# Last expert's output of a decoder layer sent off in two column halves, with first halves of four combine tiles loaded in between

## The reference, cut to what matters

```python
def run_block(args):                       # one block of 128 tokens of one expert
    tok, e = args
    xb = x_pad[tok]
    hb = jax.nn.silu(xb @ w_gate[e]) * (xb @ w_up[e])
    return hb @ w_down[e]
...
y = zeros.at[slot_tok].add(yb * slot_gate[:, None])
...
x = x + y                                  # then the final norm
return (rms_norm(yp, norm_final), rms_norm(ys, norm_final), ...)
```

## Time and profile before

| what | us |
|---|---|
| median of three runs | 1828.81 |
| lowest and highest run | 1828.12, 1834.88 |
| the profiled execution's own time | 1829.44 |
| span of its profile | 1827.8 |
| TensorE busy | 1767.3 (97%) |
| VectorE busy | 1152.3 (63%) |
| ScalarE busy | 860.0 (47%) |
| mean granted clock of TensorE | 0.983 of full speed |

### The profile page before, as it was taken

One profiled execution on the slowest core, in us unless ns is written; L12 is line 12 of the kernel. 1 busy time (PEld: TensorE's weight loads), 2 busy tenths in 40 slices (PEclk: granted clock), 3 DMA queues, 4 the chain that ended last, 5 costly groups with the idle time before them and its releaser, 6 DMA issues. The chain is left out here.

```text
span 1827.8 us, 28479 instructions
## 1 busy us (share of the span) xinstructions
PE 1767.3 (97%) x9926; PEld 1524.9 (83%) x9926; DVE 1152.3 (63%) x1954; ACT 860.0 (47%) x1554; POOL 486.5 (27%) x495
## 2 busy tenths in 40 slices
PE   7999999999999999999989999979999999999997
PEld 6878888999999788888879978768888888888882
DVE  5267666311111454545455556689999999999985
ACT  5255545311111233233232223358778777877873
POOL 3022332000000322323231112224955333332320
PEclk9999999999999999999999999979999999999998
DMA  7111212232222203030304643279999999999987
GB/s 233 48 48 47 55 47 55 86 94 70 81 70 82 66 16 92 26 92 23 95 2 143 199 146 111 85 306 386 391 389 385 392 384 384 386 381 390 384 335 291
DMA packets 149531, 333.30 MB, mean 182 GB/s; under 512 B 33712, under 2 KB 103008, under 8 KB 123792
## 3 DMA queue, kind: packets, MB, share of 16 engines
q1 hardware_dynamic: 127408, 278.19, 42.1%
q0 software_dynamic: 21376, 53.27, 8.4%
q10 hardware_dynamic: 672, 0.85, 0.3%
HBM read 304.24 MB, written 46.35 MB: 192 GB/s over the span
## 5 line engine op out<-in xcount | busy, mean ns | idle before, releaser
L2850 POOL DMA_INDIRECT y_d<-e_y,e_idxs x32 | 138.4, 4325 | 201.4 <-DVE e_y L2956 179.8
L2927 DVE TENSOR_TENSOR e_Lg<-e_rawg,e_Hg 128x1024 fp32r<-128x1024 f32 x128 | 148.2, 1219 | 8.3 <-ACT e_Hg L2876 8.3
L2927 DVE TENSOR_TENSOR e_Lu<-e_rawu,e_Hu 128x1024 fp32r<-128x1024 f32 x128 | 147.8, 1214 | 0.0
L2927 DVE TENSOR_TENSOR e_Ld<-e_rawd,e_Hd 128x1024 fp32r<-128x1024 f32 x124 | 143.1, 1214 | 0.0
L2876 ACT ACTIVATE e_Hg<-e_rawg 128x1024 fp32r<-128x1024 f32 x128 | 124.8, 1051 | 9.2 <-DMA e_rawg<-in_w_gate 9.2
L2876 ACT ACTIVATE e_Hu<-e_rawu 128x1024 fp32r<-128x1024 f32 x124 | 120.9, 1059 | 0.0
L2876 ACT ACTIVATE e_Hd<-e_rawd 128x1024 fp32r<-128x1024 f32 x124 | 120.8, 1051 | 0.0
L164 PE MATMUL bank<-r_wH,xH 128*128 128x512 f32 x256 | 105.3, 411 | 3.2 <-DVE r_gs L1530 3.2
L164 PE MATMUL bank<-e_Hg,e_xH 128*128 128x512 f32 x256 | 100.8, 394 | 3.6 <-DVE e_xL L2933 3.6
L164 PE MATMUL bank<-e_Hu,e_xH 128*128 128x512 f32 x256 | 102.8, 402 | 0.0
L166 PE MATMUL bank<-r_wH,xL 128*128 128x512 f32 x256 | 100.9, 394 | 0.0
(11 more groups left out here) (472 smaller groups left out, 4768.4 us busy)
## 6 DMA issues: line engine op xcount, KB each, us to landing
e_rawg<-in_w_gate SPq DMA_DIRECT2D x64, 1024.0 KB, 8.9
e_rawu<-in_w_up SPq DMA_DIRECT2D x64, 1024.0 KB, 7.7
e_rawd<-in_w_down SPq DMA_DIRECT2D x62, 1024.0 KB, 8.4
raw<-in_w_in SPq DMA_DIRECT2D x51, 512.0 KB, 4.0
c_Y<-y_d SPq DMA_DIRECT2D x8, 1024.0 KB, 12.6
m_t<-b_m_s POOLq DMA_DIRECT2D x8, 528.0 KB, 3.4
m_gate<-gate_t POOLq DMA_DIRECT2D x8, 528.0 KB, 3.9
m_m<-m_t POOLq DMA_DIRECT2D x8, 528.0 KB, 3.9
```

The lines of the kernel that those rows point to most:

```text
L2850: pool.indirect_dma_start(out=ch.y_d, out_offset=bass.IndirectOffsetOnAxis(ap=idx[:, e % IDX, 1:2], axis=0), in_=y[:], in_offset=None, bou ...
L2927: dve.tensor_tensor(L[kind][:, q], raw[kind][:, q], H[kind][:, q].bitcast(F32), ALU.subtract).then_inc(w_lo[kind], 1)
```

## The change

1. In the first stage, VectorE does `back(1)` before the bias sum of L423, and ScalarE waits for that sum and stores it one tile later.
2. `turn_hidden(31)` moves from behind `down(30)` to behind its first quarter; `hidden_hi(31)` and `hidden_lo(31)` move up with it, between the splits of the last down weights on VectorE. The split hidden rows of expert 31 lie in `xH`, `xL`.
3. The down product of expert 31 goes half by half into banks G and U: the 12 matmuls of the first 512 columns, then the 12 of the last.
4. VectorE computes two lists of row numbers (2r and 2r+1), and GpSimd scatters each half of `e_y` with an indirect DMA of its own (rows of 2 KB).
5. SyncE loads the first column halves of tiles 8, 0, 1 and 2 once the first half (and the scatter of expert 30) has landed, and after the second half their second halves and the five other tiles. Readers of those four tiles wait for both halves.

```diff
@@ stage_front, scalar
-                    if t == 1:
+                    if t == 2:
                         act.wait_ge(bias_sum, 1)
                         act.dma_start(ch.skew...)
@@ stage_front, vector
+                    back(t)
                     if t == 1:
                         dve.wait_ge(bias_mm, 1)
                         dve.tensor_tensor(ch.skew_rows[:], ...).then_inc(bias_sum, 1)
-                    back(t)
@@ class Combine
+    EARLY = (8, 0, 1, 2)
+    def landed(self, eng, t):
+        eng.wait_ge(self.y_in[t], 32 if t in self.EARLY else 16)
...
+        def load(t, cols):
+            m = rows_of(t)
+            sp.dma_start(self.Y[0:m, t, :, cols], ch.y_d[2 * t * P:2 * (t * P + m), cols].rearrange("(p k) d -> p k d", k=2)).then_inc(self.y_in[t], 16)
+        self.half_served(sp)
+        for t in self.EARLY:
+            load(t, slice(0, 512))
         self.served(sp)
         for t in self.ORDER:
-            sp.dma_start(self.Y[0:m, t], ch.y_d[...])
+            load(t, slice(512, D) if t in self.EARLY else slice(0, D))
@@ stage_experts
+        def hidden_at(e):
+            return (xH[:, 0:FT], xL[:, 0:FT]) if isinstance(e, int) and e == NE - 1 else (hH[:], hL[:])
...
         def served(eng):
             eng.wait_ge(y_st, 16 * NE)
+            eng.wait_ge(half_st, 16)
+        def half_served(eng):
+            eng.wait_ge(y_st, 16 * (NE - 1))
+            eng.wait_ge(half_st, 16)
...
+        sums_at = lambda e: (G, U) if isinstance(e, int) and e == NE - 1 else Y
@@ gpsimd
-                scatter(LAST)
+                pool.wait_ge(rows_done, 2)
+                for f, done, sent in ((0, y_a, half_st), (1, y_b, y_st)):
+                    pool.wait_ge(done, NE)
+                    pool.indirect_dma_start(out=ch.y_d.rearrange("r (f d) -> (r f) d", f=2), out_offset=...(ap=row2[:, f:f + 1], axis=0),
+                                            in_=y[:, f * 512:(f + 1) * 512], ...).then_inc(sent, 16)
@@ scalar
                 def out_evac(e):
-                    act.wait_ge(used["d"], e * NQ + 2 * NQ)
+                    if isinstance(e, int) and e == LAST:
+                        act.wait_ge(half_mm, 1)
+                    else:
+                        act.wait_ge(used["d"], e * NQ + 2 * NQ)
                     act.wait_ge(y_st, e * 16)
...
                         split_hi("g", NE)
+                        hidden_hi(NE - 1)
...
-                hidden_hi(NE - 1)
                 combine.diagonals(act)
@@ vector
+                def half_rows():
+                    dve.wait_ge(ch.e_idx_in[LAST % IDX], 16 * (LAST // IDX + 1))
+                    dve.tensor_copy(rowf[:], idx[:, LAST % IDX, 1:2]).then_inc(rows_done, 1)
+                    dve.wait_ge(rows_done, 1)
+                    dve.tensor_scalar(row2[:, 0:1], rowf[:], 2.0, None, ALU.mult)
+                    dve.tensor_scalar(row2[:, 1:2], rowf[:], 2.0, 1.0, ALU.mult, ALU.add).then_inc(rows_done, 1)
...
-                        split_lo("g", NE)
+                        split_lo("g", NE, range(NQ // 2))
+                        hidden_lo(NE - 1)
+                        half_rows()
+                        split_lo("g", NE, range(NQ // 2, NQ))
                     if not first:
                         out_evac(e - 1)
...
-                hidden_lo(NE - 1)
                 out_evac(NE - 1)
@@ tensor
-                def down(e, kind="d"):
+                def down(e, between=None):
...
+                        if q == 0 and between:
+                            between()
+                def down_halves(e):
+                    high, low = hidden_at(e)
+                    pe.wait_ge(h_lo, e + 1)
+                    for f in range(2):
+                        cols = slice(f * 512, (f + 1) * 512)
+                        for q in range(NQ):
+                            if f == 0:
+                                pe.wait_ge(w_lo["g"], NE * NQ + q + 1)
+                            mm = split_matmuls(pe, sums_at(e)[f][:], ...)
+                            if f == 1:
+                                mm.then_inc(used["d"], 1)
+                        if f == 0:
+                            mm.then_inc(half_mm, 1)
...
-                        down(e - 1)
+                        down(e - 1, between=None if left else lambda: turn_hidden(NE - 1))
...
-                turn_hidden(NE - 1)
-                down(NE - 1, "g")
+                down_halves(NE - 1)
```

More of the change, by code:

```diff
@@ L2617, with __init__ @@
     AHEAD = {0: 2, 2: 4, 6: 7}
-    def __init__(self, ch, sb, gain, served):
-        self.ch, self.gain, self.served = ch, gain, served
+    EARLY = (8, 0, 1, 2)
+    def __init__(self, ch, sb, gain, served, half_served):
+        self.ch, self.gain, self.served, self.half_served = ch, gain, served, half_served
         self.g_in, self.y_in, self.half, self.a_done, self.sq_done, self.ms_part, self.ms_done, self.root_done, self.rstd_done, self.o_done, self.o_st = (
@@ L2693, in weigh @@
             i = self.ON_DVE.index(t)
-            dve.wait_ge(self.y_in[t], 16)
+            self.landed(dve, t)
             dve.scalar_tensor_tensor(out=Y[:, t, 0], in0=Y[:, t, 0], scalar=gates[:, t, 0:1], in1=x2[:, t], op0=ALU.mult, op1=ALU.add).then_inc(self.half, 1)
@@ L2743, in experts @@
             m = rows_of(t)
-            pe.wait_ge(self.y_in[t], 16)
+            self.landed(pe, t)
             for f, bank in enumerate(self.halves(t)):
@@ L2786, in served @@
             eng.wait_ge(y_st, 16 * NE)
+            eng.wait_ge(half_st, 16)
+        def half_served(eng):
+            eng.wait_ge(y_st, 16 * (NE - 1))
+            eng.wait_ge(half_st, 16)
         end = ch.experts_at + 4 * 9 * NQ * 1024
         room = Room(nc, ch.experts_at, end)
-        combine = Combine(ch, room, rows, served)
+        combine = Combine(ch, room, rows, served, half_served)
         beyond = Beyond(ch, Room(nc, ch.experts_at, end), room, served)
@@ L2865, in _ @@
                         fill_beyond(e - 2)
-                scatter(LAST)
+                pool.wait_ge(rows_done, 2)
+                for f, done, sent in ((0, y_a, half_st), (1, y_b, y_st)):
+                    pool.wait_ge(done, NE)
+                    pool.indirect_dma_start(out=ch.y_d.rearrange("r (f d) -> (r f) d", f=2), out_offset=bass.IndirectOffsetOnAxis(ap=row2[:, f:f + 1], axis=0),
+                                            in_=y[:, f * 512:(f + 1) * 512], in_offset=None, bounds_check=4 * T - 1, oob_is_err=False).then_inc(sent, 16)
                 pool.wait_ge(scat2, 16 * 2 * NT)
@@ L2884, in hidden_hi @@
                     act.wait_ge(h_turned, e + 1)
-                    act.activation(hH[:].rearrange("p k i -> p (k i)"), HT[:], ACT.Copy).then_inc(h_hi, 1)
+                    act.activation(hidden_at(e)[0].rearrange("p k i -> p (k i)"), HT[:], ACT.Copy).then_inc(h_hi, 1)
                 def gate_sigmoid(e):
@@ L2892, in out_evac @@
                 def out_evac(e):
[L2893 removed]
+                    if isinstance(e, int) and e == LAST:
+                        act.wait_ge(half_mm, 1)
+                    else:
+                        act.wait_ge(used["d"], e * NQ + 2 * NQ)
                     act.wait_ge(y_st, e * 16)
[L2895 removed]
+                    act.activation(y[:, 0:512], sums_at(e)[0][:], ACT.Copy).then_inc(y_a, 1)
                 def body(e, first, left):
@@ L2923, in _, with split_lo @@
             def _(dve):
-                def split_lo(kind, e):
-                    for q in range(NQ):
+                def split_lo(kind, e, qs=range(NQ)):
+                    for q in qs:
                         dve.wait_ge(w_hi[kind], e * NQ + q + 1)
@@ L2937, in hidden_lo @@
                     dve.wait_ge(h_hi, e + 1)
-                    dve.tensor_tensor(hL[:].rearrange("p k i -> p (k i)"), HT[:], hH[:].rearrange("p k i -> p (k i)").bitcast(F32),
-                                      ALU.subtract).then_inc(h_lo, 1)
+                    high, low = (x.rearrange("p k i -> p (k i)") for x in hidden_at(e))
+                    dve.tensor_tensor(low, HT[:], high.bitcast(F32), ALU.subtract).then_inc(h_lo, 1)
+                def half_rows():
[4 more added lines that the diff above has]
+                    dve.tensor_scalar(row2[:, 1:2], rowf[:], 2.0, 1.0, ALU.mult, ALU.add).then_inc(rows_done, 1)
                 def gate_product(e):
```

12 lines of the change are left out of this document (7 added, 5 removed).

## The result

The changed kernel takes 1835.42 us (median of 18 runs, 1833.78 to 1839.1) against 1832.97 for the kernel before in the same comparison (18 runs, 1828.12 to 1836.51). The ratio of the comparison is 1.0018, 95% interval 1.0012 to 1.0025: slower by 3.3 us, give or take 1.2, which is within 0.5%. (The ratio is estimated from all the runs and need not be the quotient of the medians, which is 1.0013, or 2.45 us, here.) The forecast was 1830.8 us, so the time lies above the forecast range, whose top was 1833.4. The sign of the small change was right. Its size and the base that it was added to were not.

What follows compares the result with a forecast made beforehand. TensorE, busy 97% of the span, was taken as the bound, with the end set by VectorE's last stretch from T. Sum: 1829.44 - 0.8 (first stage) + 2.2 (T) = 1830.8 us; range 1827.2 to 1833.4.

Steps and rivals of the forecast that it cites:

- The base: Starting time of the sum: the profiled execution's own 1829.44 us, 0.63 above the median of the runs.
- I take no loss: Tail loads: 2 KB rows run as fast as whole ones, so tile 8's second half lands 7.2 us behind the start.
- T: VectorE's start on tile 1's squares, opening its unbroken end stretch; forecast 2.2 us later; S is SyncE's first load issue.
- First stage: Start of the kernel: TensorE's 0.81 us wait for xL of tile 1 goes, gaining 0.8 us.
- Turn of expert 31 and VectorE's lateness: Before the tail: turn inside down(30) removes a gap worth 1.65 us; VectorE's moved steps delay expert 30's scatter to 1780.75.
- Start of the loads: Behind the first half's scatter: loads start at 1788.4 instead of 1790.6 on the old clock, 2.2 us earlier.
- short rows are slow: Rival on the tail loads: half loads run at 333 GB/s, T 1.2 us later, time 1832.0; chance 0.1.
- TensorE's wait: Between residuals and tile 8 in the tail: TensorE idles 3.4 us, where it idled 0.49 before.
- The clock: TensorE's tail: tile 8 takes 5.55 us, three instructions fast and five slow; tile 1 takes 6.1 us in low clock.
- cold all the way: Rival in the tail: tiles 8 and 1 both wholly at 1.2 GHz, T +4.2, time 1832.8; chance 0.2.
- The mechanism: Tail: the 2.2 us gain at the scatter is spent on the queue ahead of tile 8 and a colder TensorE.
- the halves pay: Rival in the tail: TensorE keeps 2.4 GHz through tile 8, time 1827.2; chance 0.25 for everything below 1829.4.

Runs made afterwards that it cites:

- experiment 5: Changed kernel with all 13 loads after both half scatters, each tile's two halves one behind the other; 1829.67 us, ratio 0.9994 to the kernel before.
- 8: Changed kernel with nine whole loads, none early, and tile 5's residual laid between tile 8's matmuls; 1832.68 us, ratio 1.0003 to the kernel before.
- Experiment 4: Changed kernel with tile 5's residual products made three times more ahead of the real ones (12 matmul instructions); 1832.99 us, ratio 1.001 to the kernel before.
- experiments 6: Changed kernel with nine whole loads, none early, and tile 0 loaded ahead of tile 8; 1831.46 us, ratio 1.0001 to the kernel before.
- experiment 2: Changed kernel with no early loads: nine whole loads behind both half scatters; 1831.33 us, ratio 1.0000 to the kernel before.
- experiment 3: Changed kernel with the same 13 loads in the same order, all only after both half scatters; 1837.41 us, ratio 1.0035 to the kernel before.
- 9: Changed kernel with only tile 0's first half loaded early; 1830.29 us, ratio 0.9996 to the kernel before.
- 10: Changed kernel with only the first halves of tiles 8 and 0 loaded early; 1830.05 us, ratio 0.9990 to the kernel before.
- experiment 7: Changed kernel with all 13 loads after both half scatters, early tiles cut by expert row (4 KB rows) instead of columns; 1836.17 us, ratio 1.0024 to the kernel before.

## Why the prediction was wrong, and where it was right

The forecast failed in two terms: the base of 1829.44 us, and the loads, where "I take no loss" put tile 8's second half at 7.2 us behind the first issue. It took 9.7, and the granted clock fell before tile 8 began.

**The base.** The sum stood on the profiled execution's 1829.44 us, and that was taken to be 0.63 above the median. That median was of three runs. Over 18 runs it is 1832.97, and single runs go from 1828.12 to 1836.51. Of the miss of 4.6 us, 3.53 is this base and 1.05 the difference: 1.4 was forecast (2.2 less 0.8), and the medians are 2.45 apart. The highest of the three runs, 1834.88, was in view and was left aside. A profile gives no better base. In ten of the twelve kernels profiled here the profiled execution lies below its kernel's median, by up to 4.4 us, and in the other two within 0.1 us of it. The spread goes with the clock: in the 32 runs of the kernel before beside experiments 5 to 8, the eight with a mean granted clock of 0.981 average 1833.6 us, and the nine with 0.983 average 1830.6. Which stretch of the kernel ran at the lower clock in the longer runs no trace shows, since each kernel has one profile.

**The size.** In the ratio it is +3.3 us, and the interval (2.2 to 4.6 us) leaves the forecast +1.4 outside. The profiled pair shows where it came from, and there the forecast was further off: T moved by 6.35 us, against 2.2 less 0.8.

- *First stage, -0.8.* The wait went. At expert 31 the profile of the edit alone has all of the gain (0.83 us), that of the changed kernel 0.22; in the time it does not show (1.0004, with 0.9996 at the interval's end).
- *Turn of expert 31 and VectorE's lateness.* Right. On the new clock (forecast less 0.8) the turn was due at 1773.15 and came at 1773.74; expert 30's scatter was due at 1779.95 and came at 1780.23; the first copy of `e_y`, held by that scatter, at 1783.2 and came at 1783.90. GpSimd's two issues were due at 1784.6 and 1785.85 and came at 1785.33 and 1786.61. Of the 0.3 to 0.8 us by which these came late, up to 0.6 is the gain of the first stage that this trace lacks. The gap of 0.3 us between them is in the chain.
- *Start of the loads.* Due at 1787.6, it came at 1788.01: 2.6 us before the old kernel's, as against 3.0.
- *The loads.* This is the step of the mechanism that failed most: tile 8's second half was reckoned at 7.2 us behind the start, with loads of 2 KB rows as fast as whole ones and SyncE at 0.43 us per issue. It took 9.7, with 0.59 to 0.69 us for each of the first five issues. "I take no loss" was wrong, and so was the rival "short rows are slow" in its size: 1.2 us was its price, 2.5 was measured. The reason given against that rival was a misreading of the earlier trace rows. Here are the two stretches of the first stage with their packets:

```profile
DMA packets 406, 0.67 MB, mean 333 GB/s; under 512 B 80, under 2 KB 90, under 8 KB 406
DMA packets 227, 0.82 MB, mean 412 GB/s; under 512 B 26, under 2 KB 26, under 8 KB 227
```

The first line is 10 to 12 us, the second 14 to 16. Without the small packets, 316 carry 0.67 MB in the first, 2 KB each; in the second 201 carry 0.82 MB, 4 KB each. The stretch at 412 GB/s was the loads of `in_x_prompt`, whose rows are 4 KB, and the stretch of 2 KB rows was that at 333. So the row did not speak against the rival. The Trainium skill, page "DMA: Bandwidth & Descriptors", section "Bandwidth", asks for at least 1 MiB in a DMA and has 341 GB/s for 1 MB, measured with DMAs issued from GpSimd. By that rate the estimate is 2.9 + 5.4 = 8.3 us. The trace is beyond it, and adjacent halves of the same size (experiment 5) made no measurable loss, so the rule alone does not decide the time either.

- *TensorE's wait.* Forecast 3.4 us, measured 4.20: later data, partly hidden by residuals that took 8.92 us and not 7.22.
- *The clock.* Forecast 5.55 us for tile 8 and 6.1 for tile 1. They took 7.0 and 6.6. This is the rival "cold all the way", which was given 0.2 and priced at 6.8 each. Its condition came true: the granted clock was at 0.50 from about 1797.1, and tile 8's second half landed at 1797.74. The forecast had three of tile 8's eight instructions at full clock; none was. Experiment 4 shows that the clock made these durations: with more work ahead, the same 16 matmuls took 8.91 us.

The forecast's T on the new clock was 1807.9. It came at 1812.81, 4.9 us later: 2.9 from tile 8's start (0.4 from the start of the loads, 2.5 from the transfer), 1.5 from tile 8, and 0.5 from tile 1. That sums the profile. The two profiles differ by 6.0 us and the medians by 2.45, since the trace before lay 3.5 us below its kernel's median and the trace after at its own. So the 6.35 us of T are more than the change costs in most executions. The same is seen in experiments 6 and 8, where 3.8 and 4.2 us of T - S against experiment 2's one profile (itself 3.3 us below its median) came to nothing that the times could show. That the clock's fall moves from one execution to the next would explain this, and the spread of the mean granted clock fits it; it is not shown for this stretch.

**The mechanism** was forecast. Shown in the times are the order of the queue (experiments 3 against 5), the early loads as the whole loss (2), and a shorter queue as the cure (9, 10). The cold TensorE behind the wait is shown in the profiles (4); how much of the loss in time it is, the runs don't part from noise. The rival "the halves pay" fell: its condition, a clock kept through tile 8, never held with four early tiles.

**Left open.** Why the half loads are as slow as they are at their start. Row length gives about half of the excess in one pair of profiles (experiment 7). In a running queue it costs little: in the changed kernel the second halves of tiles 1 and 2 landed 1.35 us behind the one before, where half of a whole load is 1.25, while the first half of tile 2 landed 2.5 us behind that of tile 1. The issue cost on SyncE is no full answer either: tile 8's second half was issued 2.7 us behind the first load, and the load ahead of it, issued 0.7 us earlier, was still on its way 6.4 us after that. With 4 KB rows (experiment 7) the issues were as fast as whole ones, and it still took 8.95 us. The second scatter's writes are no cause: in experiment 3 they were done, and the loads were no faster.

## What to carry to other kernels

Before an input is divided to start its load early, look at which piece the next in-order engine takes first, and count every byte and every issue that the early pieces put ahead of it on the same queue. Here an early start of 0.7 us put 1.5 MB of three other tiles, which TensorE did not need yet, ahead of tile 8. Keep the early part as short as the time it fills. Before a rate is taken from another stretch of the trace, check what its transfers look like: the packet count and the bytes give their size. When runs spread by more than the change is worth, one profiled execution says what can happen and not what the median does: take more runs before choosing a base.

## What the hardware showed that was not expected

- In the first five issues a half load in rows of 2 KB cost SyncE 0.59 to 0.69 us (experiment 3, and the changed kernel), one in rows of 4 KB 0.33 to 0.43 (experiment 7), as much as a whole load with rows of 8 KB (0.33 to 0.45 before). Later issues of the long queues took up to 2.05 us (experiment 3).
- A run of half loads starts slowly: 1.75 MB took 9.7 and 10.7 us from the first issue with 2 KB rows and 8.95 with 4 KB rows, where whole loads had 1.25 MB after 5.9 us. Later on, halves of 0.5 MB came 1.35 us apart.
- Behind twelve added matmul instructions, in time that the engine spent waiting anyway, the next 16 took 8.91 us instead of 13.60: the granted clock stayed at 1.00 through the first of the two tiles (until 1803).
- The same 16 residual products took 7.22 us in one profile and 8.87 to 8.92 in nine others, of kernels with the same code there.
- The second half's scatter took 2.09 us in the chain (forecast 3.0), but expert 30's whole one took 3.59, more than the 3.19 of the earlier trace rows.
